# Expert weights laid out by partition, and loaded in 4 MB and 8 MB transfers instead of 2 MB ones

## The reference

```python
def moe_ffn(h, w_router, b_router, w_gate_up, b_gate_up, w_down, b_down):
    ...
    top_v, top_e = lax.top_k(logits, TOP_K)
    gates = jax.nn.softmax(top_v, axis=-1)
    ...
    def expert_block(args):
        tok, e = args
        xb = x_ext[tok]
        gu = jnp.dot(xb, w_gate_up[e]) + b_gate_up[e]
        gate = jnp.minimum(gu[:, :D_FF], SWIGLU_LIMIT)
        up = jnp.clip(gu[:, D_FF:], -SWIGLU_LIMIT, SWIGLU_LIMIT)
        act = gate * jax.nn.sigmoid(SWIGLU_ALPHA * gate) * (up + 1.0)
        return jnp.dot(act, w_down[e]) + b_down[e]
```

## Time and profile before

| | |
|---|---|
| median of 3 runs | 1054.86 us (1054.58 to 1055.35) |
| span of the profiled execution | 1053.5 us |
| TensorE busy | 1037.2 us (98%) |
| VectorE, ScalarE, GpSimd busy | 197.8, 143.2, 5.5 us |
| moved by DMA | 424.62 MB, mean 403 GB/s |
| first gate-up product of expert 0 | at 156.23 us |

### The profile page before, as it was taken

The page is one execution under the profiler, slowest core; times in us unless marked ns, Lnnn a source line. Parts: engine busy times, 40 slices in busy tenths (PEclk is TensorE's granted clock), DMA queues, the critical chain, the costliest instruction groups (busy, mean ns, idle before and its releaser), DMA issues.

```text
span 1053.5 us, 12013 instructions
## 1 busy us (share of the span) xinstructions
PE 1037.2 (98%) x4815; PEld 388.1 (37%) x4815; DVE 197.8 (19%) x500; ACT 143.2 (14%) x300; POOL 5.5 (1%) x23
## 2 busy tenths in 40 slices
PE   9999999999999999999999999999999999999998
PEld 5655543333333333333333333333333332333333
DVE  2162232111111111111111111111111111011111
ACT  2144431101111100110111111111110110001101
POOL 1000000000000000000000000000000000000000
PEclk9999999999999999999999999999999999999999
DMA  9964699999999999999999999999999999999997
GB/s 337 363 236 160 258 373 400 428 429 428 428 429 429 428 429 428 428 429 428 428 429 429 429 429 429 428 429 428 428 429 429 429 429 428 429 428 428 425 425 292
DMA packets 42699, 424.62 MB, mean 403 GB/s; under 512 B 6545, under 2 KB 7609, under 8 KB 17337
## 3 DMA queue, kind: packets, MB, share of 16 engines
q1 hardware_dynamic: 42376, 423.84, 96.1%
q10 hardware_dynamic: 304, 0.53, 0.1%
HBM read 423.31 MB, written 1.05 MB: 403 GB/s over the span
## 4 chain that ended last, share of the span: by engine, by line
PE 80%; DMA 11%; SPq 8%; issue 0%; DVE 0%; POOL 0%; ACT 0%; POOLq 0%
PE bank L1597 32%; PE bank L1633 17%; DMA ring<-in_w_gate_up 9%; PE bank L1199 7%; SPq L391 5%; PE bank L1508 4%; PE bank L1558 4%; SPq L398 3%; PE bank L1393 3%; PE bank L1446 2%; PE bank L1519 2%; PE bank L1617 2%; DMA ring<-in_w_down 2%; PE bank L1235 1%; PE bank L1608 1%; SPq L535 1%
## 5 line engine op out<-in xcount | busy, mean ns | idle before, releaser
L1597 PE MATMUL bank<-ring,xe_t 128*64 128x512 f32 x2048 | 449.4, 594 | 8.2 <-DMA ring<-in_w_gate_up 7.5
L1597 PEld LDWEIGHTS bank<-ring,xe_t 128*64 128x64 f32 x2048 | 143.1, 137 | 310.9 <-issue 289.9
L1633 PE MATMUL bank<-ring,late 128*64 128x512 f32 x992 | 219.9, 595 | 0.0
L1633 PEld LDWEIGHTS bank<-ring,late 128*64 128x64 f32 x992 | 68.5, 137 | 127.2 <-issue 122.0
L1118 DVE TENSOR_SCALAR gate_c<-bank 128x512 f32<-128x512 f32 x32 | 22.1, 692 | 436.6 <-PE bank L1597 436.6
L780 ACT ACTIVATE s_sb<-bank 128x256 f32<-128x256 f32 x32 | 12.3, 383 | 459.4 <-PE bank L1608 459.4
L1199 PE MATMUL bank<-ring 128*128 128x512 f32 x160 | 72.0, 596 | 0.5 <-issue 0.5
L1558 PE MATMUL bank<-late,s_sb 64*128 64x512 f32 x248 | 61.6, 615 | 0.0
L1508 PE MATMUL bank<-xres,pick 128*64 128x512 f32 x248 | 60.0, 605 | 0.0
L796 ACT ACTIVATE late<-bank 128x512 f32<-128x512 f32 x31 | 18.5, 597 | 218.9 <-PE bank L1633 218.9
L1116 DVE COPY row_of<-fold 128x64 f32 x31 | 6.1, 195 | 197.0 <-PE bank L1446 197.0
(11 more groups left out here) (214 smaller groups left out, 429.6 us busy)
## 6 DMA issues: line engine op xcount, KB each, us to landing
ring<-in_w_gate_up SPq DMA_DIRECT2D x124, 2048.0 KB, 35.8
ring<-in_w_down SPq DMA_DIRECT2D x59, 2048.0 KB, 32.8
ring<-in_w_in SPq DMA_DIRECT2D x5, 2048.0 KB, 14.9
ring<-in_w_gate_up SPq DMA_DIRECT2D x8, 1024.0 KB, 24.7
ring<-in_w_down SPq DMA_DIRECT2D x6, 1024.0 KB, 29.2
ring<-in_w_out SPq DMA_DIRECT2D x2, 2048.0 KB, 10.6
ring<-in_w_down SPq DMA_DIRECT2D x7, 512.0 KB, 22.2
ring<-in_attn_bias SPq DMA_DIRECT2D x1, 1536.0 KB, 18.2
```

The source lines that it names most:

```text
L1597: mm = pe.matmul(bank[h][c * CAP:(c + 1) * CAP, :], xe_t[:, k, :], w[:, k % RUN, at:at + BANK], start=False, stop=(k == KD - 1), skip_grou ...
L1633: mm = pe.matmul(dst[c * CAP:(c + 1) * CAP, :], turned[:, at:at + CAP], w[:, k % DRUN, c * BANK:(c + 1) * BANK], start=(k == 0), stop=(k = ...
```

## The change

On the host the weights are laid out anew ahead of the launch (`expert_layout`): all that one partition gets of an expert's gate-up (64 KB) lies in one run, as does all that it gets of its down matrix (32 KB). The contents of the ring are the same as before. What changes:

- Experts 0 to 4, 30 and 31 are still loaded in pieces of 2 MB. Their runs of 16 KB now lie 64 KB apart (gate-up) or 32 KB apart (down).
- Experts 5 to 14 are loaded in three transfers of 4 MB with runs of 32 KB: two for gate-up, one for down.
- Experts 15 to 29 are loaded in two transfers: 8 MB with runs of 64 KB for gate-up, 4 MB with runs of 32 KB for down.
- A merged transfer is issued when the last of the pieces that it overwrites is used, and TensorE waits once for all of it (`signals_of`, `signals_through`).
- Half of the last piece's words change places, so that its parts are runs of up to 4 KB; `last_product` reads them where they now lie.
- TensorE's program holds experts 0 to 4 written out, a loop of 5 turns over 5 to 14, one of 7 turns over 15 to 28, and 29 to 31 as before.

```diff
+SINGLE = 5
+PAIR_LAPS = 5
+WHOLE = SINGLE + LAP * PAIR_LAPS
+WHOLE_LAPS = (NE - 3 - WHOLE) // LAP
+HALVES = 2
...
+def by_pairs(n):
+
+    return SINGLE <= n < NE - 2
...
+def signals_of(n, k):
+
+    if by_pairs(n):
+        return int(k in ((0, GUN) if n >= WHOLE else (0, 2, GUN)))
+    return 2 if n == HALVES and k in IN_HALVES else 1
...
+def signals_through(n, k):
+
+    s = piece_of(n, k)
+    return sum(signals_of(*nk) for i, nk in enumerate(LOAD_ORDER[:TURN_OF[n, k] + 1]) if i % PIECES == s)
...
             def load_gu(e, h, s):
-                sp.dma_start(gu_half(s), w_gate_up[0, e, h * RUN * P:(h + 1) * RUN * P, :].rearrange("(p j) n -> p j n", j=RUN))\
-                    .then_inc(ld_piece[s], 16)
+                sp.dma_start(gu_half(s), gu_rows(e, h)).then_inc(ld_piece[s], 16)
...
+            def load_gu_pair(e, q, s):
+                sp.dma_start(ring[:, s * PIECE:(s + 2) * PIECE].rearrange("p (o n) -> p o n", o=1),
+                             w_gate_up[e].rearrange("p j n -> p (j n)")[:, q * 2 * PIECE:(q + 1) * 2 * PIECE]
+                             .rearrange("p (o n) -> p o n", o=1)).then_inc(ld_piece[s], 16)
+
+            def load_gu_whole(e, s):
+                sp.dma_start(ring[:, s * PIECE:(s + GUN) * PIECE].rearrange("p (o n) -> p o n", o=1),
+                             w_gate_up[e].rearrange("p j n -> p (j n)").rearrange("p (o n) -> p o n", o=1))\
+                    .then_inc(ld_piece[s], 16)
+
+            def load_d_pair(e, s):
+                sp.dma_start(ring[:, s * PIECE:(s + 2) * PIECE].rearrange("p (o n) -> p o n", o=1),
+                             w_down[e].rearrange("p j n -> p (j n)").rearrange("p (o n) -> p o n", o=1))\
+                    .then_inc(ld_piece[s], 16)
...
+            def next_pairs(base, far, n):
+
+                if n >= WHOLE:
+                    used, count = free_of(base, n, GUN - 1)
+                    sp.wait_ge(used, count + GUN * far)
+                    load_gu_whole(far + n, piece_of(n, 0))
+                else:
+                    for q in range(GUN // 2):
+                        used, count = free_of(base, n, 2 * q + 1)
+                        sp.wait_ge(used, count + GUN * far)
+                        load_gu_pair(far + n, q, piece_of(n, 2 * q))
+                used, count = free_of(base, n, KINDS - 1)
+                sp.wait_ge(used, count + DN * far)
+                load_d_pair(far + n, piece_of(n, GUN))
...
-                with sp.Fori(0, LAP * (LAPS - 1), LAP) as far:
-                    for n in range(3, 3 + LAP):
-                        next_gu(base, far, n)
-                        next_d(base, far, n)
...
+                for n in range(3, SINGLE):
+                    next_gu(base, n)
+                    next_d(base, n)
+                with sp.Fori(0, LAP * PAIR_LAPS, LAP) as far:
+                    for n in range(SINGLE, SINGLE + LAP):
+                        next_pairs(base, far, n)
+                with sp.Fori(0, LAP * WHOLE_LAPS, LAP) as far:
+                    for n in range(WHOLE, WHOLE + LAP):
+                        next_pairs(base, far, n)
+                for n in range(WHOLE + LAP * WHOLE_LAPS, NE - 2):
+                    next_pairs(base, 0, n)
...
                 for i, (lo, hi, h) in enumerate(LAST_PARTS):
-                    cols = slice(h * BANK, (h + 1) * BANK)
-                    sp.dma_start(down_piece(s)[:, lo:hi, cols], rows[:, lo:hi, cols]).then_inc(ld_last[i - 1] if i else ld_piece[s], 16)
+                    words = slice((h * DRUN + lo) * BANK, (h * DRUN + hi) * BANK)
+                    sp.dma_start(last_piece[:, words], rows[:, words]).then_inc(ld_last[i - 1] if i else ld_piece[s], 16)
...
-                    if k % RUN == 0:
-                        halves = int(n >= 2 and s in IN_HALVES)
-                        pe.wait_ge(ld_piece[s], 16 * (PIECE_LOADS[s] * round_no + LOADS_A_LAP * lap + loads_before(n, k // RUN) + halves) + 16)
+                    if k % RUN == 0 and signals_of(n, k // RUN):
+                        pe.wait_ge(ld_piece[s], 16 * (PIECE_SIGNALS[s] * round_no + lap) + 16 * signals_through(n, k // RUN))
...
                 expert(base, 0, 0, round_no, meanwhile)
-                with pe.Fori(0, LAPS) as lap:
-                    for n in range(1, 1 + LAP):
+                for n in range(1, SINGLE):
+                    expert(base, 0, n, round_no)
+                with pe.Fori(0, PAIR_LAPS) as lap:
+                    for n in range(SINGLE, SINGLE + LAP):
+                        expert(base, lap, n, round_no)
+                with pe.Fori(0, WHOLE_LAPS) as lap:
+                    for n in range(WHOLE, WHOLE + LAP):
                         expert(base, lap, n, round_no)
```

More of the change, by code:

```diff
@@ L53 @@
 LAST = NE - 1 - LAP * LAPS
-LOADS_A_LAP = KINDS * LAP // PIECES
+SINGLE = 5
[3 more added lines that the diff above has]
+HALVES = 2
 TINT = (1, 0)
@@ L95, in piece_of @@
     return TURN_OF[n, k] % PIECES
[L98 to L104, removed]
+def by_pairs(n):
+    return SINGLE <= n < NE - 2
+IN_HALVES = (0, 1, GUN)
+def signals_of(n, k):
[5 more added lines that the diff above has]
+    return sum(signals_of(*nk) for i, nk in enumerate(LOAD_ORDER[:TURN_OF[n, k] + 1]) if i % PIECES == s)
+PIECE_SIGNALS = [sum(signals_of(*nk) for i, nk in enumerate(LOAD_ORDER) if i % PIECES == s) for s in range(PIECES)]
 END_PARTS = {(NE - 2, 0): (0, 2), (NE - 2, 1): (0, 2, 3), (NE - 1, 0): (0, 1, 3)}
@@ L389, in _, with gu_rows, d_rows @@
         def _(sp):
+            def gu_rows(e, h):
+                return w_gate_up[e, :, h * RUN:(h + 1) * RUN, :]
+            def d_rows(e, c):
+                return w_down[e, :, c * DRUN:(c + 1) * DRUN, :]
             def load_gu(e, h, s):
-                sp.dma_start(gu_half(s), w_gate_up[0, e, h * RUN * P:(h + 1) * RUN * P, :].rearrange("(p j) n -> p j n", j=RUN))\
-                    .then_inc(ld_piece[s], 16)
+                sp.dma_start(gu_half(s), gu_rows(e, h)).then_inc(ld_piece[s], 16)
             def load_d(e, c, s, cuts=(0,)):
-                rows = w_down[0, e, c * DRUN * P:(c + 1) * DRUN * P, :].rearrange("(p j) n -> p j n", j=DRUN)
+                rows = d_rows(e, c)
                 for lo, hi in zip(cuts, cuts[1:] + (DRUN,)):
@@ L491, in third @@
                     s = piece_of(n, h)
-                    rows = w_gate_up[0, n, h * RUN * P:(h + 1) * RUN * P, :].rearrange("(p j) n -> p j n", j=RUN)
+                    rows = gu_rows(n, h)
                     sp.wait_ge(gu_row_used, 2 * round_no + h + 1)
@@ L500, in third @@
                 s = piece_of(n, GUN)
-                rows = w_down[0, n, 0:DRUN * P, :].rearrange("(p j) n -> p j n", j=DRUN)
+                rows = d_rows(n, 0)
                 sp.wait_ge(d_rows_used, round_no + 1)
@@ L511, in weights @@
                 third(base, round_no)
[L512 to L518 removed]
+                for n in range(3, SINGLE):
[9 more added lines that the diff above has]
+                    next_pairs(base, 0, n)
                 for n in (NE - 2, NE - 1):
[L520 removed]
+                    next_gu(base, n, GUN - 1)
                     s = piece_of(n, GUN - 1)
[L522 removed]
+                    rows = gu_rows(n, GUN - 1)
                     used, count = free_of(base, n, GUN - 1)
@@ L1742, in experts @@
                     add_residual()
-                for n in range(NE - LAST, NE - 2):
+                for n in range(WHOLE + LAP * WHOLE_LAPS, NE - 2):
                     expert(base, 0, n, round_no)
@@ L1771, with expert_layout @@
         'mh_norm_g', 'w_out', 'norm2_g', 'w_router', 'b_router', 'w_gate_up', 'b_gate_up', 'w_down', 'b_down']
+def expert_layout(w_gate_up, w_down):
+    gate_up = np.asarray(w_gate_up)[0].reshape(NE, GUN, P, RUN, 2 * FF).transpose(0, 2, 1, 3, 4)
+    down = np.asarray(w_down)[0].reshape(NE, DN, P, DRUN, D).transpose(0, 2, 1, 3, 4).copy()
+    last = down[NE - 1, :, DN - 1].reshape(P, DRUN, 2, BANK).transpose(0, 2, 1, 3)
+    down[NE - 1, :, DN - 1] = last.reshape(P, DRUN, D)
+    return {"w_gate_up": gate_up.reshape(NE, P, KD, 2 * FF), "w_down": down.reshape(NE, P, DN * DRUN, D)}
 def kernel(**inputs):
@@ L1779 @@
     arrays, args = {}, []
-    given = [(name, np.ascontiguousarray(inputs[name])) for name in _INS] + [("attn_bias", attention_bias())]
+    laid = expert_layout(inputs["w_gate_up"], inputs["w_down"])
+    given = [(name, np.ascontiguousarray(laid.get(name, inputs[name]))) for name in _INS] + [("attn_bias", attention_bias())]
     for name, a in given:
```

36 lines of the change are left out of this document (20 added, 16 removed).

## The result

The changed kernel takes 1058.85 us (1058.22 to 1059.57, 5 runs) beside 1054.86 for the kernel before: a ratio of 1.0037, with an interval of 1.0025 to 1.0048. Forecast were 1058.4 us, slower, and a range of 1055.0 to 1064.8. The profiled execution has a span of 1057.2 us (1053.5 before).

A forecast was written before the change was run, and what follows sets the result against it. Late in the kernel loads (29.37 us an expert) bind over TensorE (27.52). Later start +4.3 us, waits gone at the end -0.8: +3.5 on span 1053.5 gives 1057.0, with 1.4 to the median 1058.4 us; range 1055.0 to 1064.8.

The forecast's parts named there:

- The bound: Kernel before: loads take 29.37 us an expert, TensorE 27.52; the loads' lead is used up near expert 24.
- The price of a merge: Merging 2 MB loads in experts 5 to 29 saves 0.067 us a merge, 6.0 us over 90 merges.
- The wait: Experts 15 to 29 wait for all 8 MB; lead ends about expert 19, expert 29 begins 4.3 us later, at 970.3.
- What I left out of the sum: Perhaps seven more instruction packets than 12, each blocking one DMA engine under 1 us: up to 0.6 us, not summed.
- The residual: Its 1.91 us on TensorE before expert 29, claimed to be hidden in the wait for the 8 MB.
- The tail: From expert 30 to the end no wait for a load is left: 0.8 us saved, between 0.4 and 1.1.
- The sum: Whole kernel: +4.3 - 0.8 = +3.5 us, span 1057.0, median 1058.4, slower by 0.33%; chance 0.62.
- No saving (1064.3): Longer runs save nothing in the loads; expert 29 begins at 976.2, +9.4 us, 1064.3; chance 0.12.
- Slower reading of rows 64 KB apart: Experts 0 to 4, 30 and 31 read slower; at 1% less, 8.1 us more, 1066.5; chance 0.10.
- Faster through a higher rate per byte: Experts 5 to 29: long runs move bytes faster; at 437 GB/s 14.4 us saved, 1050.3; chance 0.08.
- The DMA engines running dry: At the change to pairs, expert 5: 1 to 3 us more, 1059.4 to 1061.4; chance 0.08.
- The margin there: At expert 5's first pair, loads still queued cover the later issue by 3 us, less what some engines are ahead.

The follow-up runs named there:

- the run that changed the wait: The kernel before, old layout and 2 MB pieces, but TensorE waits for all four gate-up pieces before starting experts 15 to 29: 1064.02 us.
- the shorter pairs kernel: The changed kernel with 4 MB pairs for experts 5 to 29, no 8 MB transfers, experts 1 to 4 and 5 to 28 in loops: 1051.64 us.
- the run with short runs: The changed kernel with the same transfers and waits, but gate-up in its first layout, so in 16 KB runs: 1063.11 us.
- the changed plan with the shorter program: The changed kernel with experts 1 to 4 in a loop instead of written out: 1057.53 us.
- The pairs: The changed kernel with 4 MB pairs for experts 5 to 29: 1052.84 us, or 1051.64 with 1 to 4 and 5 to 28 in loops.
- the runs in pieces: The changed kernel with all loads in 2 MB pieces: 1056.21 us; the kernel before with TensorE's program as long as the changed kernel's: 1056.6 us.
- the run from expert 3: The shorter pairs kernel with the first merged load at expert 3 instead of 5: 1053.37 us.
- the mixed plan: The changed kernel with 8 MB transfers only for experts 15 to 18, pairs for 19 to 26, 2 MB pieces for 27 to 29: 1054.63 us, repeated 1054.85.
- the mixed plan with the shorter program: The mixed plan with experts 1 to 4 in a loop and the residual added ahead of expert 27: 1051.22 us.

## Why the prediction was right, step by step

*The bound.* Right. Loads of 29.37 us an expert behind a TensorE of 27.52 meant that the end hangs on the landing of the last experts' weights plus TensorE's work behind them, and the run that changed the wait moved the end by 8.9 us, where 9.4 were forecast.

*The price of a merge.* Right in kind, a little undersized. The changed kernel steps by 29.07 us, 0.30 for four merges, 0.074 us each where I took 0.067; the shorter pairs kernel steps by 941.15 - 912.01 = 29.14, 0.23 for three. The short runs' windows in the kernel before had given 0.090 as the upper bound, too high as argued. By the ceiling of 435.2 GB/s in the Trainium skill ("DMA: Bandwidth & Descriptors", "Where 436 GB/s comes from") it could be 0.075 at most, an estimate from that page. The trace agrees: the merged loads move at 433 GB/s in the 200 us above. That transfers in themselves cost nothing (the run with short runs) was assumed in the sum and is now shown.

*The wait.* Right. Its own price, 10.2 us less what falls away at the end, was forecast as 9.4 and measured as 8.9 (with three more instruction packets in it). The lead ends at expert 19 as worked out, and expert 29 begins at 971.0 for 970.3.

*What I left out of the sum.* The instruction packets: 12 became 19, as guessed, but they cost 1.1 to 1.6 us and not up to 0.6. In the sum this took back what the larger price of a merge gave: 85 merges ahead of expert 28's gate-up at 0.074 are 6.3 us, and its landing moved by only 946.83 - 941.59 = 5.24. One step of the guess is plainly off: a packet is in the way of its engine for more than "less than 1 us". Between 246 and 258 us of the changed kernel the one of q8 is booked with 0.6% of 16 x 12 us, 1.2 us, while by 9,600 us of engine time for 257.11 MB 16 KB of data take 0.6 us.

```profile
q8 instruction: 1, 0.02, 0.6%
```

But the cost doesn't go by their number. From 158 to 946 us, where a packet can delay the landing for expert 28, there are 3 in the kernel before, 7 in the changed plan with the shorter program and 9 in the changed kernel:

```profile
q8 instruction: 3, 0.05, 0.0%
```
```profile
q8 instruction: 7, 0.11, 0.1%
```
```profile
q8 instruction: 9, 0.15, 0.1%
```

With 7 of them expert 28 gets its weights 946.83 - 940.18 = 6.65 us earlier than before, all that the 85 merges give and more; with 9 of them 1.1 us of it is gone. The pairs show the same: 71 merges at 0.075 are 5.3 us, of which 946.83 - 941.15 = 5.68 arrive with 5 packets and 946.83 - 942.66 = 4.17 with 9. So two and four more cost nothing that the landings show, six more cost 1.1 us in these two pairs of runs. In the runs in pieces, with 9 as well, the products on expert 28's last piece start at 947.26 (new layout) and 948.19 (old), 0.4 and 1.4 us later than before. Each of these figures is from one execution, and why they differ so is open.

*The residual.* Wrong by 0.35 us. The forecast let the wait hide it. TensorE's own 27.51 + 1.91 = 29.42 us from expert 28 to 29 is longer than the loads' 29.07, so here alone no wait stands ahead of the product.

*The tail.* Undersized: 0.8 us taken, 1.4 measured. From expert 29's start to the end of the span are 87.5 us before (1053.5 - 966.02) and 86.1 after (1057.2 - 971.08 in the chain of waits). Expert 30's gate-up gives 0.3 of it (14.27 to 13.95). The way from expert 31's gate-up to the 48 short products gives 0.4 (1039.57 - 1014.28 = 25.29 before, 1043.91 - 1019.03 = 24.88 after), of which the gap of 0.15 was counted. The short products give 0.4 (5.80 to 5.40). The other 0.25 or so lies behind TensorE's last product, where the forecast had no term.

*The sum.* + 5.1 - 1.4 = + 3.7 us of span, forecast + 4.3 - 0.8 = + 3.5. The sizes erred by up to 1 us and in both directions; that the total is off by only 0.45 us in the median is partly luck. Of these 0.45 us 0.25 lie between span and median (1058.85 - 1057.2 = 1.65, where the forecast took the 1.4 of the kernel before).

*The rivals.* No saving (1064.3): refuted by the rate, and close to what short runs in merged transfers give (1063.1), which is the condition it named. Slower reading of rows 64 KB apart: refuted, by two kernels of one program length and two layouts (1056.21 and 1056.6). For the row pitches at large powers of two, from 512 KB on, of which the Trainium skill speaks ("DMA: Bandwidth & Descriptors", "Latency and other measured facts") that says nothing; the pitch here is 64 KB. Faster through a higher rate per byte: refuted, 433 GB/s at 64 KB runs. The DMA engines running dry: not at expert 5, as worked out, and real from expert 3, each us dry at its full price. The changed kernel's window behind the issue for expert 5 has the engines fully busy (the share can pass 1.00 because packets count where they start):

```profile
246.00:252.00 6.00, 6.00 (x30) 2.01 (x28) 0.00 (x0) 0.00 (x0) 0.00 (x0) 1.00 1.04 444
```

The margin there was probably larger than the 3 us of the forecast, which put the whole 2.7 us of a transfer's overhead ahead of its first byte. In the run from expert 3 the new packets start at about 192.25, 1.0 us after the issue.

## What to carry to other kernels

A longer transfer saves time only through its longer runs, but it takes away the head start that separate semaphores give: price both, the saving as packets removed times their overhead, the loss as the landing time of all but the first piece. Where loads bind only late, it stands to reason to merge in the stage where the compute engine is still the slower one and to keep small transfers where it waits; the mixed plan does so, but its gain over pairs throughout isn't clear of the noise. Keep every issue ahead of the end of the queue, since an idle DMA engine was not made up for later here (1.7 us at the end for a gap at 191 us). Unrolling a program to fit such stages can have a price of its own, 1.1 to 1.6 us for six more bodies here.

The best kernels of the study are the mixed plan with the shorter program (1051.22 us) and pairs from 5 to 29 with the shorter program (1051.64), both 0.3% under the kernel before. Their intervals overlap.

## What was not expected of the hardware

- Seven more instruction packets of 16 KB cost 1.1 to 1.6 us, though they carry 0.1 MB, 0.3 us at the full rate. The profile counts them in the share of the same 16 engines. One is booked on its engine with 1.2 us, twice the time of 16 KB of data. Why some programs pay for them and others, with three or five more, don't is open; which engine each hits wasn't told apart.
- What looks like a wait for the program's own instructions can come behind the last branch, 0.63 us in one execution and 3.04 in another, and the mean TensorE clock is lower in the second (0.997 for 0.999), with 0.61 in the window behind the wait. Which length or position of the program brings it is open: one of two programs of nearly the same plan has it.
